# Three edits to the expert layer of a one-core transformer kernel: who makes the weight remainders of the second pass, how many expert slots stand between two heads, and where one block of gates lies

## The reference

```python
q = (h @ w_pq).reshape(B, S, 8, 2, 128)
sc = einsum("bshcd,hcnd->bshcn", q, sub_keys)          # 128 keys on each of two sides
s_top, i_top = top_k(sc, 16)
cand = s_top[..., 0, :, None] + s_top[..., 1, None, :]  # 16 x 16 sums
best, pos = top_k(cand, 16)                             # 16 experts per head and token
gate = softmax(best)
a = gelu(einsum("ced,cd->ce", u_emb[idx], h))           # idx = key1 * 128 + key2
out = einsum("ce,ced->cd", gate * a, v_emb[idx])
```

## Time and profile before

| | |
|---|---|
| runs | 3264.32, 3267.0 and 3268.2 us; median 3267.0 |
| the profiled execution | 3261.49 us, of which the span of the instructions is 3259.7 |
| granted TensorE clock, mean | 0.991 |
| PE, DVE, ACT, POOL busy | 96%, 69%, 37%, 39% of the span |
| the heads, first slot to last scores | about 503 to 733 us |
| other u slots | about 733 to 1285 us |
| second pass | about 1285 to 1885 us |

### The profile page before, as it was taken

The page is one execution under the profiler, slowest core; times in us unless marked ns, Lnnn a source line. Parts: engine busy times, 40 slices in busy tenths (PEclk is TensorE's granted clock), DMA queues, the critical chain, the costliest instruction groups (busy, mean ns, idle before and its releaser), DMA issues.

```text
span 3259.7 us, 42914 instructions
## 1 busy us (share of the span) xinstructions
PE 3122.5 (96%) x16170; PEld 2700.5 (83%) x16170; DVE 2252.7 (69%) x3332; ACT 1217.1 (37%) x1818; POOL 1271.7 (39%) x635
## 2 busy tenths in 40 slices
PE   7999999998999998999999999999999999999998
PEld 5877778998989898988888978888588888888886
DVE  7899868998888885998998863204487666522105
ACT  3334543233333333333333353323436564333225
POOL 0010144552344444888888634442020001444432
PEclk9999999999999999999999999999999999999999
DMA  3211133444899999888898722223122222322222
GB/s 126 94 61 46 59 123 123 134 133 155 293 323 338 330 333 345 308 322 318 310 325 314 262 91 97 97 96 126 59 85 72 78 78 78 120 100 97 97 91 91
DMA packets 172859, 548.15 MB, mean 168 GB/s; under 512 B 16825, under 2 KB 41913, under 8 KB 172529
## 3 DMA queue, kind: packets, MB, share of 16 engines
q1 hardware_dynamic: 107968, 380.10, 33.3%
q0 software_dynamic: 36864, 134.23, 12.2%
q10 hardware_dynamic: 27824, 31.08, 2.7%
HBM read 490.60 MB, written 54.55 MB: 167 GB/s over the span
## 4 chain that ended last, share of the span: by engine, by line
PE 61%; DVE 19%; DVEq 9%; DMA 4%; issue 2%; ACTq 2%; ACT 2%; POOL 1%; SPq 0%; POOLq 0%
PE ps L212 41%; PE ps L1111 7%; PE ps L1506 6%; DVEq L1432 4%; DMA experts_back<-experts_dram 3%; DVE conv_out L760 2%; ACTq L1187 2%; DVE gated_lo L1425 1%; DMA ring<-in_stream 1%; PE ps L1086 1%; DVEq L747 1%; ACT slot_parts L196 1%; DVE slot_parts L200 1%; PE ps L1785 1%; DVE h_rows L1439 1%
## 5 line engine op out<-in xcount | busy, mean ns | idle before, releaser
L200 POOL TENSOR_TENSOR slot_parts<-ring,slot_parts 128x1024 fp32r<-128x1024 f32 x362 | 902.6, 2495 | 1332.8 <-ACT slot_parts L196 1332.2
L212 PE MATMUL ps<-h_norm_hi,slot_parts 128*128 128x512 f32 (+1 forms) x4576 | 1361.5, 374 | 54.0 <-DVE slot_parts L200 41.9
L212 PEld LDWEIGHTS ps<-h_norm_hi,slot_parts 128*128 128x128 f32 x4576 | 851.9, 189 | 172.6 <-DVE slot_parts L200 46.2
L212 PE MATMUL ps<-x_low,slot_parts 128*128 128x512 f32 (+1 forms) x2224 | 813.0, 366 | 0.0
L196 ACT ACTIVATE slot_parts<-ring 128x1024 fp32r<-128x1024 f32 x560 | 589.7, 1053 | 484.5 <-DMA ring<-in_stream 315.6
L1111 PE MATMUL ps<-gated_hi,slot_parts 128*128 128x384 f32 x2048 | 549.0, 339 | 36.4 <-DVE gated_lo L1425 24.6
L200 DVE TENSOR_TENSOR slot_parts<-ring,slot_parts 128x1024 fp32r<-128x1024 f32 x198 | 242.8, 1226 | 345.4 <-ACT slot_parts L196 345.1
L212 PEld LDWEIGHTS ps<-x_low,slot_parts 128*128 128x128 f32 x2224 | 422.1, 190 | 49.0
L1111 PEld LDWEIGHTS ps<-gated_hi,slot_parts 128*128 128x128 f32 x2048 | 371.9, 188 | 70.1 <-issue 52.9
L1111 PE MATMUL ps<-gated_lo,slot_parts 128*128 128x384 f32 x1024 | 342.9, 335 | 0.0
L1417 DVE TENSOR_TENSOR gated<-gates_back,experts_back 128x384 f32<-128x384 f32 x128 | 226.3, 1769 | 57.3 <-DMA experts_back<-experts_dram 50.6
(11 more groups left out here) (434 smaller groups left out, 4075.2 us busy)
## 6 DMA issues: line engine op xcount, KB each, us to landing
ring<-in_stream SPq DMA_DIRECT2D x560, 512.0 KB, 3.5
experts_dram<-experts SPq DMA_DIRECT2D x64, 384.0 KB, 5.8
gates_dram<-gates_by_key ACTq DMA_DIRECT2D x24, 1024.0 KB, 18.5
gates_back<-gates_dram SPq DMA_DIRECT2D x32, 768.0 KB, 6.0
experts_back<-experts_dram SPq DMA_DIRECT2D x64, 384.0 KB, 6.0
x_res<-in_xT SPq DMA_DIRECT2D x4, 512.0 KB, 8.2
x_res<-in_xT SPq DMA_DIRECT2D x1, 2048.0 KB, 8.3
v_row<-in_stream,pick_table POOLq DMA_INDIRECT x128, 6.9
```

Of the source, the lines that this page charges most:

```text
L200: e.tensor_tensor(to[:, BUFFER[n], 1, :], ring[:, n % RING, :], to[:, BUFFER[n], 0, :].bitcast(F32), ALU.subtract).then_inc(s_lo, 1)
L212: mm = e.matmul(psum, w2[wv][:, k, :], x2[xv], start=start and v == 0, stop=stop and v == 2)
```

## The change

Three things. (1) In the second pass VectorE calls `slot_lo` for every slot, in its turn j right after the low part of `gated`(j-1) and ahead of the weighted sum; GpSimd makes none there and only issues the gathers. (2) `UH` is 5: seven slots per head, so 40 u slots stand in the heads and 88 behind; `TURN` becomes u44, the groups spread over u45 to u120 (76 slots in place of 84), the dots over u56 to u125 (70 in place of 78). (3) The sixth block of gates isn't sent to DRAM: it stays in `W_out` (buffer 1), which in the second pass no longer may be overlaid. The gates come back as 640 KB in place of 768, and `gated` is made by two instructions, 320 columns from `gates_back` and 64 from the kept block. To make room the six v row buffers lie where `h_norm` and `x_low` were, so that the first gather waits for the last u product (`slot_done` >= `n_v`) rather than for the last gates to be in DRAM.

```diff
@@ -21,7 +21,7 @@
 TAPS = 31
 HEADS, HD = 16, 64
 PH, NKEY, TOPK = 8, 128, 16
-UH = 4
+UH = 5
 WT, WBLK = 4, 64
 HOTS, GBUF = 4, 3
 SETS = ((0, 128, 1),)
@@ -45,7 +45,7 @@
 
 STREAM = [
     ("glu", 16), ("q", 8), ("kv", 3), ("gates", 16), ("attn_o", 8), ("conv_out", 8), ("w_out", 8),
-    ("peer_heads", 48), ("peer_u", 96), ("peer_v", 128),
+    ("peer_heads", (2 + UH) * PH), ("peer_u", NKEY - UH * PH), ("peer_v", 128),
     ("f1_in", 44), ("f1_out", 22),
     ("misc", 1), ("ik", 1), ("iq", 4), ("dkv", 1), ("gqk", 8), ("gv", 8), ("wide2", 24),
     ("dsa", 16), ("dsa_out", 8), ("mix_out", 8),
@@ -925,6 +925,7 @@
 
     m = ExitStack()
     BLOCKS = SD // WBLK
+    SPILLED = BLOCKS - 1
     keep(m, 2)
     gate_left = sb(m, "gate_left", [P, 2, S])
     iota_b = sb(m, "iota_bf16", [P, P], BF16)
@@ -957,13 +958,12 @@
     with ExitStack() as sc:
         W_out = sb(sc, "gates_by_key", [P, 2, NKEY, WBLK])
     with ExitStack() as sc:
-        W_in = sb(sc, "gates_back", [P, 2, BLOCKS, 4, WBLK])
+        W_in = sb(sc, "gates_back", [P, 2, SPILLED, 4, WBLK])
         A_in = sb(sc, "experts_back", [P, 2, 2, SD])
         GV = sb(sc, "gated", [P, GBUF, SD])
         G_hi, G_lo = [sb(sc, "gated_" + x_, [P, GBUF, SD], F32R) for x_ in ("hi", "lo")]
-        v_rows = [sb(sc, f"v_row{x_}", [P, D]) for x_ in range(ROWS_V)]
     with ExitStack() as sc:
-        sb(sc, "peer_before_rows", [P, max(2 * NKEY * WBLK, 2 * 4 * SD + 4 * SD + 3 * GBUF * SD + ROWS_V * D)])
+        sb(sc, "peer_before_rows", [P, 2 * NKEY * WBLK])
         h_rows = [sb(sc, f"h_rows{x_}", [P, D]) for x_ in range(len(SETS))]
         row_0 = sb(sc, "u_row0", [P, D])
         pick_tab = sb(sc, "pick_table", [P, 3, STEPS])
@@ -975,9 +975,11 @@
     u_rows = [row_0[:, :], gate_left[:, :, :].rearrange("p v s -> p (v s)"),
               norm_sq[:, :, :].rearrange("p v s -> p (v s)"), norm_rs[:, :, :].rearrange("p v s -> p (v s)")]
     h_again = [x_.rearrange("p (k s) -> p k s", k=KT) for x_ in (u_rows[0], u_rows[2])]
+    v_rows = [(H, Lo32)[x_ // 4][:, x_ % 4 * 2:x_ % 4 * 2 + 2, :].rearrange("p a s -> p (a s)") for x_ in range(ROWS_V)]
+    W_kept = W_out[:, SPILLED % 2, :, :]
     row_sum = h_rows
     g2 = T[:, 2, :, :].rearrange("p n (h k) -> p (n h) k", k=TOPK)
-    W_dram = nc.dram_tensor("gates_dram", (NKEY // 4, P, BLOCKS, 4, WBLK), F32, kind="Internal").ap()
+    W_dram = nc.dram_tensor("gates_dram", (NKEY // 4, P, SPILLED, 4, WBLK), F32, kind="Internal").ap()
     A_dram = nc.dram_tensor("experts_dram", (NKEY // 2, P, 2, SD), F32, kind="Internal").ap()
 
     p_keys, p_ev, p_sc, p_top = sems("peer_", "keys", "evacuated", "scores", "top")
@@ -1004,7 +1006,7 @@
     for _h in range(PH):
         BEFORE_V += [("q", 2 * _h), ("q", 2 * _h + 1)] + [("u", UH * _h + _j) for _j in range(UH)]
     BEFORE_V += [("u", _j) for _j in range(UH * PH, NKEY)]
-    n_own = n_p + 6 * PH + 5
+    n_own = n_p + (2 + UH) * PH + 5
     TURN = UH * PH + 4
     UNNORMED = 4
     GROUPS = SD // WT
@@ -1181,7 +1183,7 @@
                     e.wait_ge(w_mm, g + 1)
                     e.activation(view(W_out[:, b % 2, 0, g % PER * WT:], [WBLK, NKEY], [1, WT]),
                                  view(PS[:, 4 + g % 4, :], [1, NKEY], [P, WT]), ACT.Copy).then_inc(w_ev, 1)
-                    if g % PER == PER - 1:
+                    if g % PER == PER - 1 and b < SPILLED:
                         e.wait_ge(w_ev, g + 1)
                         for c in range(4):
                             e.dma_start(W_dram[8 * c:8 * c + 8, :, b, :, :].rearrange("g p i t -> p g (i t)"),
@@ -1221,22 +1223,15 @@
 
         def v_row(s):
             after(e, r_sum, R_MANY + s - ROWS_V + 1 if s >= ROWS_V else 0)
-            e.indirect_dma_start(v_rows[s % ROWS_V][:, :], None, experts_v, pick(1, s))\
+            e.indirect_dma_start(v_rows[s % ROWS_V], None, experts_v, pick(1, s))\
                 .then_inc(rv_in[s % ROWS_V], 16)
 
         for s in range(STEPS):
             u_row(s)
         e.wait_ge(r_dot, R_MANY + STEPS)
-        for b in range(2):
-            e.wait_ge(w_out[b], 64 * ((BLOCKS + 1 - b) // 2))
-        for s in range(ROWS_V):
+        e.wait_ge(slot_done, n_v)
+        for s in range(STEPS):
             v_row(s)
-        e.wait_ge(s_lo, ORDINAL[n_v])
-        for n in range(n_v, n_v + NKEY - 2):
-            slot_lo(e, n)
-            for s in sums_after(n - n_v - 1):
-                if s + ROWS_V < STEPS:
-                    v_row(s + ROWS_V)
         leave(e)
 
     def peer_sp_back(e, j):
@@ -1244,7 +1239,7 @@
         g = j // 4
         if j == 0:
             for x_ in range(2):
-                e.wait_ge(w_out[x_], 64 * ((BLOCKS + 1 - x_) // 2))
+                e.wait_ge(w_out[x_], 64 * ((SPILLED + 1 - x_) // 2))
         if j % 4 == 0:
             after(e, v_g, 4 * (g - 1))
             e.dma_start(W_in[:, g % 2, :, :, :].rearrange("p b i t -> p (b i t)"),
@@ -1414,9 +1409,13 @@
                 if j % 2 == 0:
                     e.wait_ge(a_in[j // 2 % 2], 16 * (j // 4 + 1))
                 after(e, v_lo, j - GBUF + 1)
-                e.tensor_tensor(GV[:, j % GBUF, :].rearrange("p (b t) -> p b t", t=WBLK),
+                far = SPILLED * WBLK
+                e.tensor_tensor(GV[:, j % GBUF, 0:far].rearrange("p (b t) -> p b t", t=WBLK),
                                 W_in[:, g % 2, :, j % 4, :],
-                                A_in[:, j // 2 % 2, j % 2, :].rearrange("p (b t) -> p b t", t=WBLK), ALU.mult)\
+                                A_in[:, j // 2 % 2, j % 2, 0:far].rearrange("p (b t) -> p b t", t=WBLK), ALU.mult)
+                if j == 0:
+                    e.wait_ge(w_ev, GROUPS)
+                e.tensor_tensor(GV[:, j % GBUF, far:], W_kept[:, j, :], A_in[:, j // 2 % 2, j % 2, far:], ALU.mult)\
                     .then_inc(v_g, 1)
             if j:
                 i = j - 1
@@ -1424,6 +1423,7 @@
                 e.wait_ge(v_hi, i + 1)
                 e.tensor_tensor(G_lo[:, i % GBUF, :], GV[:, i % GBUF, :], G_hi[:, i % GBUF, :].bitcast(F32),
                                 ALU.subtract).then_inc(v_lo, 1)
+                slot_lo(e, n_v + i)
                 if j == 2:
                     e.wait_ge(r_dot, R_MANY + STEPS + 1)
                     e.wait_ge(r_spread, R_SPREAD)
@@ -1433,15 +1433,12 @@
                     e.wait_ge(rv_in[s % ROWS_V], RV_IN[s % ROWS_V] + 16 * (s // ROWS_V + 1))
                     total = row_sum[set_of(s)]
                     if s in STEP0:
-                        e.tensor_scalar(total[:, :], v_rows[s % ROWS_V][:, :], row_gate[:, s:s + 1], None, ALU.mult)\
+                        e.tensor_scalar(total[:, :], v_rows[s % ROWS_V], row_gate[:, s:s + 1], None, ALU.mult)\
                             .then_inc(r_sum, 1)
                     else:
-                        e.scalar_tensor_tensor(out=total[:, :], in0=v_rows[s % ROWS_V][:, :],
+                        e.scalar_tensor_tensor(out=total[:, :], in0=v_rows[s % ROWS_V],
                                                scalar=row_gate[:, s:s + 1], in1=total[:, :], op0=ALU.mult,
                                                op1=ALU.add).then_inc(r_sum, 1)
-                if i >= NKEY - 2:
-                    e.wait_ge(s_lo, ORDINAL[n_v + i])
-                    slot_lo(e, n_v + i)
         leave(e)
         for d in range(KT):
             if d < KT - 1:
```

## The result

The changed kernel takes 3286.2 us (median of 4 runs, 3282.42 to 3292.05), against 3265.66 us for the kernel before: 1.006 times, 95% interval 1.0037 to 1.0083. It is 20 us slower, where 26 us less were forecast. The profiled execution took 3282.42 us, its span is 3280.2. Behind the second pass the two traces are within 1.1 us of each other (1374.7 us before, 1373.6 after).

A forecast was written before the change was run, and what follows sets the result against it. TensorE was taken to be fed too late, in the second pass by a 4.5 us ring of GpSimd, VectorE and ScalarE. First part +3, pass -29, total -26: 3261.5 to 3235.5, or 3241 us for the median; range 3214 to 3262.

The forecast's parts named there:

- The exclusion of VectorE and GpSimd: Second pass: `gated` takes 0.55 us, but 2.75 where GpSimd is in a `slot_lo`; moving the rests to VectorE ends this.
- The ring of 4.5 us a slot: Second pass before: GpSimd's `slot_lo`, VectorE's `gated` and ScalarE's parts follow each other, 4.5 us against TensorE's 4.16.
- the chain behind the activations' load: Second pass: issue, landing and VectorE's work take 9.1 us behind gates, 0.75 late in one turn of four.
- rival D: Second pass: loads slower by a microsecond or more, chain 10.4 us, nothing gained there; 3261 to 3270 us, chance 0.12.
- My upper bound of 600 us: Second pass with loads 1.3 us slower: 18.7 us for four slots, 600 for the pass, change 0.
- five spills, some 7.7 each. They stay.: Stretch behind the heads: 38.7 us over both engines' work was put down to five spills and kept unchanged.
- Heads +34: Heads: eight added u slots at 4.21 us each make them 34 us longer.
- `TURN` -4: At `TURN`: one more slot covers 4.2 us of TensorE's 9.1 us wait, -4 us, bounds 0 and -4.2.
- the sixth spill: Ahead of the second pass: without this spill, its 13.80 us issue and the low clock go, -12 us.
- its 415 over the 396: Stretch behind the heads, 430.7 us before: 415 taken; 396 if VectorE catches up in spills, 420 if it can't.
- The kept block: Second pass: the second piece of `gated` adds 0.1 us a turn; 0.2 more would be 6 us.
- E: Before the second pass: VectorE makes the kernel slower if over 11.8 us are bare per spill; 3276 us, chance 0.08.

The follow-up runs named there:

- E4: E3 with VectorE's low part and rest of slot j-1 put ahead of `gated`(j) and its wait for activations; 3194.87 us, ratio 0.978.
- E6: E3 with SyncE issuing each load of gates two slots sooner, VectorE's order unchanged; 3205.3 us, ratio 0.9805.
- E3: The changed kernel with four u slots in a head (UH = 4) in place of five; 3248.72 us, ratio 0.994.
- E8: The kernel before with only the kept block, two-piece `gated` and moved row buffers, GpSimd still making the second pass's rests; 3266.14 us, ratio 1.0006.
- E5: E3 with the dots beginning eight slots later, so that they lie in 70 slots; 3267.16 us, ratio 1.0011.
- E10: The changed kernel with the dots beginning eight slots sooner, with u48, so in 78 slots; 3270.47 us, ratio 1.0005.
- E1: The kernel before with only five u slots in a head (UH = 5); 3294.52 us, ratio 1.0074.
- E2: The kernel before with only VectorE making the second pass's rests, in the changed kernel's place; all gates spilled; 3283.81 us, ratio 1.0038.
- E7: E4 with the four DMAs of a spilled block issued one per slot, not all at once; 3172.85 us, ratio 0.9711.
- E9: E7 with five u slots in a head; 3196.44 us, ratio 0.9772.
- E11: E7 with E6's edit, the loads of gates issued two slots sooner; 3173.71 us, ratio 0.9699.
- E12: E11 with the dots beginning six slots sooner, with u42, so in 84 slots; 3168.7 us, ratio 0.9689.

## Why the prediction was wrong

**The exclusion of VectorE and GpSimd, and its end: right.** The ring of 4.5 us a slot is gone, VectorE is busy 78 us less in the pass, and its `gated` never waits for GpSimd.

**The second pass, 571 us forecast, 603.4 measured: the term mis-sized is the chain behind the activations' load.** I had the mechanism and its place, and took 0.95 us of loss in four slots and 8 us beside it, 4 for the first gathers and 4 for longer landings. It is (54.8 + 14.1) / 32 = 2.2 with these in it; ahead of slot 3, at the start, 4.4 were lost. Three parts. First, the landing behind gates took 6.9 us in the mean (31 loads after the first, from issue to landing) where I took 6.4, near a median of all 64 loads; in the kernel before, the loads behind gates alone had a mean of 6.6. Second, the count must begin at the start of slot j-3's first weight load, and the activations' load is issued not 0.42 but 0.79 us behind that (at 1448.68; the gates' load ahead of it at 1448.25). Together the chain is 0.79 + 6.9 + 0.1 + 2.3 = 10.1, and 1.8 is lost where I had 0.75. Third, slot j is late too: the ring load behind gates and activations lands up to 12 us after its issue, another 0.44 in four slots, which I didn't cost at all. The others, 0.2 in my sum, lost next to nothing. E4 and E6 took this chain apart from both ends and gained 50 and 42 us. My rival D named the chain at 10.4 us as the point where nothing is gained; it had a chance of 0.12, and in the pass it is what happened (+3.8 us). My upper bound of 600 us was also added up wrongly: 18.7 us for four slots are 600 already without the 8 us of extras.

**The first part, +3 forecast, +17.8 measured: the step that failed is "five spills, some 7.7 each. They stay."** Heads +34 and `TURN` -4 were near: 34.4 and -5.5. The stretch from `TURN` was to lose 16 + 12 - 1 = 27 us and lost 11. By the table, eight slots fewer take 34 from it (without any loss it is 457.9 us before and 423.7 after) and the sixth spill 12, so the forecast left room for 19 us of new losses, and there were 35. Some 19 of these are small losses (27.6 against 8.3), VectorE's turn of 5.31 against TensorE's 4.96, which is the size that the forecast had for them (its 415 over the 396 of a VectorE that catches up). The other 16 are at the spills: 48.8 us in five where the first five before lost 33.0 (and the five of E3, E4, E6 and E8 25 to 34). They did not stay; ScalarE was held 75 us by them in place of 57.

Why the holds are longer is open. I had thought of the row traffic beside a VectorE without slack, and the runs don't bear that out: with four slots in a head and the dots packed denser (E5) the holds took 58 us, with five and the dots spread as before (E10) still 73, and with five in the kernel before (E1) 73 in the first five. They go with the fifth slot and not with the dots' density. What the denser groups of gates cost, by themselves, was not tried. The small losses do go with the dots' density: 12 us more in E5 than in E3, 15 less in E10 than in the changed kernel.

The windows of the earlier trace rows were also read wrongly: 816.8 us is where u44 starts, not u48, so that the 430.7 us held four slots without dots. From u48 to u126 are 439.7 us, with six spills in them. Put right, my bounds of 396 and 420 become 394 and 418, and the reading explains at most 3 of the 16 us. The dots' stretch, for which I had 415, took 428.6 (866.2 to 1294.8), with VectorE busy for 362 of them, 84% and not over 92.

**The kept block: right, in its place.** In the profile of E8 the stretch ahead of the pass was 13 us shorter, forecast 12. Its second piece of `gated` was forecast at 0.1 us and adds 0.09 (below). What it would cost in E8, where the ring of GpSimd and VectorE stands, was in no sum of mine.

**The rival on the other side.** E had VectorE before the second pass as the cause of a slower kernel. 17.8 of the 21.6 us do lie there, but it wanted 11.8 us bare per spill with a pass of 571. The spills lost (40.4 + 8.4) / 5 = 9.8. Neither D nor E alone would have done it; I gave each its own chance and none to both.

**Two runs that I can't fully explain.** The pass of E2 took 37 us more than that of E3, which has 128 KB less in each gates' load, later gathers and no spill just ahead; which of these does it is open. And E1's pass was 7 us longer than before.

## What to carry to other kernels

An instruction that moves to another engine takes its place behind all that this engine waits for. Count the chain through the wait ahead of it, from the event that issues the load, with the whole of each landing's spread, before counting the busy time that it frees; where the needed work doesn't depend on the wait, put it ahead: that was worth 54 us here (E3 to E4). And when the same work is packed into fewer slots, compare each engine's turn with the slot, including the slack in which stalls were made good. Large DMAs issued back to back from an engine's queue held that engine for 51 us in E4; one per slot (E7) held it for 18, in pieces of at most 6.7, and was 22 us faster.

## What the runs showed of the hardware that I had not expected

Four 1 MB DMAs of 1 KB rows, issued back to back, hold ScalarE's queue for 5 to 18 us. The first takes 0.4 and the second 0.6 to 2.5; the third and fourth take most of it, up to 11.9 us for one. Issued a slot apart, most take 0.37, but the third or fourth of a block can still take 2.5 to 9.0 (E7, E9, E11, E12).

Over 5 us of such a hold the core's DMA engines moved 403 GB/s (window 890 to 895 above), and over the 100 us from 867 to 967 in E7 377; the DMA shares shown for them are 1.04 and 1.01, so the windows count up to 4% too much. The prediction took 358 GB/s per core for HBM from the Trainium skill (DMA: Bandwidth & Descriptors, section Bandwidth) as a limit, and found 356 in line with it; the section gives it for both cores of a pair streaming at once. For this kernel, on one core, the measurement decides: 358 was no limit. The trace before had it already, with 411 GB/s from 868 to 888. The pass itself went at 323 to 330 GB/s in E4, E6, E7, E9, E11 and E12.

A VectorE product of two float32 inputs with 64 columns adds 0.14 us from start to start (1455.83 to 1455.97) and one with 320 columns 0.41; the 384 in one piece were 0.46. So the cut costs 0.09.
